# The high halves of k and q made on GpSimd instead of ScalarE, in the attention of a hybrid pooling and attention block

## The reference, cut to what is computed

```python
D_MODEL, SEQ, CHUNK, HEAD_DIM, N_HEADS, LEFT_CHUNKS = 1024, 4096, 64, 64, 8, 8
h = rms_norm(x, norm_gain)                       # x: (1, 4096, 1024) float32
proj = einsum('bsd,de->bse', h, w_in)            # w_in: 1024 x 3072
pool_v, pool_g, q, k, v, attn_g = split(proj)    # 512 columns each
y_pool = multiscale_pool(pool_v, pool_w, pool_scale) * silu(pool_g)
# each chunk of 64 queries reads its own chunk of keys and the 8 before it
s = einsum('bqhd,bkhd->bhqk', qb, kb) / 8 + bias[clip(rel, -64, 64)]
y_attn = einsum('bhqk,bkhd->bqhd', softmax(s), vb) * silu(attn_g)
x = x + einsum('bse,ed->bsd', concat([y_pool, y_attn]), w_out)
out = rms_norm(x, final_norm_gain)
```

## Time and profile before

| | |
|---|---|
| time, median of 3 runs | 1745.24 us (1744.5 to 1748.08) |
| the profiled execution | 1741.65 us, span of its instructions 1739.9 us |
| TensorE matmuls busy | 1629.3 us (94%) |
| VectorE busy | 1057.1 us (61%) |
| ScalarE busy | 837.8 us (48%) |
| GpSimd busy | 693.5 us (40%) |
| mean granted TensorE clock | 0.979 of full |

### The profile page before, as it was taken

The page is one execution under the profiler, slowest core; times in us unless marked ns, Lnnn a source line. Parts: engine busy times, 40 slices in busy tenths (PEclk is TensorE's granted clock), DMA queues, the critical chain, the costliest instruction groups (busy, mean ns, idle before and its releaser), DMA issues. The chain is left out here.

```text
span 1739.9 us, 44264 instructions
## 1 busy us (share of the span) xinstructions
PE 1629.3 (94%) x17920; PEld 1221.2 (70%) x17920; DVE 1057.1 (61%) x2188; ACT 837.8 (48%) x1580; POOL 693.5 (40%) x734
## 2 busy tenths in 40 slices
PE   5999899999999999999967999999999999999986
PEld 2554445558676767777746878898888888888864
DVE  7776587647565556544344665666656666656664
ACT  5554455422121212111124666667666666766674
POOL 3535355311111212000413455555555555555553
PEclk8999999999999999999987999999999999999998
DMA  5665574661634442442834434544434444345331
GB/s 205 217 216 183 209 249 161 221 248 50 219 106 142 175 159 84 161 179 102 230 100 146 135 93 132 151 127 124 126 98 141 145 122 126 104 121 150 96 126 49
DMA packets 131201, 257.87 MB, mean 148 GB/s; under 512 B 15512, under 2 KB 61096, under 8 KB 128952
## 3 DMA queue, kind: packets, MB, share of 16 engines
q1 hardware_dynamic: 127896, 250.07, 43.8%
q10 hardware_dynamic: 2064, 3.67, 0.6%
q0 software_dynamic: 1040, 1.31, 0.4%
HBM read 151.33 MB, written 83.48 MB: 135 GB/s over the span
## 5 line engine op out<-in xcount | busy, mean ns | idle before, releaser
L2089 POOL TENSOR_TENSOR stages<-stages 128x512 f16<-128x512 f32 (+2 forms) x368 | 366.3, 999 | 399.9 <-ACT stages L1925 399.7
L1557 PE MATMUL bank<-middle,weights 128*128 128x128 f16 x1792 | 311.2, 219 | 1.2 <-DVE entry L1213 0.9
L1560 PE MATMUL bank<-middle,weights 128*128 128x128 f16 x1792 | 311.1, 219 | 0.0
L1559 PE MATMUL bank<-middle,weights 128*128 128x128 f16 x1792 | 311.0, 219 | 0.0
L1919 ACT ACTIVATE stages<-bank,log_ps 128x512 f32<-128x512 f32 (+2 forms) x368 | 221.6, 602 | 152.3 <-PE bank L1812 72.9
L1759 DVE CUSTOM_DVE_ANT_0 stages<-bank,stages 128x640 bf16<-128x640 f32 (+4 forms) x256 | 198.2, 774 | 77.2 <-PE bank L1724 77.2
L982 PE MATMUL bank<-middle 128*128 128x256 f16 x784 | 215.3, 275 | 7.4 <-DVE stages L1122 7.4
L984 PE MATMUL bank<-middle 128*128 128x256 f16 x784 | 215.3, 275 | 0.0
L985 PE MATMUL bank<-middle 128*128 128x256 f16 x784 | 215.3, 275 | 0.0
L1925 ACT ACTIVATE stages<-stages 128x512 f16<-128x512 f32 (+2 forms) x368 | 202.8, 551 | 11.7
L1789 PE MATMUL bank<-entry,stages 128*128 128x512 f16 x768 | 188.2, 382 | 2.5 <-DVE stages L1980 2.5
(11 more groups left out here) (147 smaller groups left out, 3611.3 us busy)
## 6 DMA issues: line engine op xcount, KB each, us to landing
entry<-in_x SPq DMA_DIRECT2D x64, 512.0 KB, 3.7
h_ops<-middle SPq DMA_DIRECT2D x16, 1792.0 KB, 6.2
middle<-h_ops SPq DMA_DIRECT2D x112, 256.0 KB, 3.0
middle<-h_ops SPq DMA_DIRECT2D x49, 512.0 KB, 7.0
middle<-middle SPq DMA_DIRECT2D x384, 64.0 KB, 2.0
residual<-entry SPq DMA_DIRECT2D x32, 512.0 KB, 3.1
entry<-residual SPq DMA_DIRECT2D x30, 512.0 KB, 4.2
out<-entry SPq DMA_DIRECT2D x30, 512.0 KB, 4.2
```

The source lines that it names most:

```text
L1557: nc.tensor.matmul(dst, wh, hop3[:, o, 0, kt, :], start=(kt == 0 and s < 2 and pair == 0), stop=False, skip_group_check=True)
L1559: nc.tensor.matmul(dst, wh, hop3[:, o, 1, kt, :], start=False, stop=False, skip_group_check=True)
L1560: mm = nc.tensor.matmul(dst, wl, hop3[:, o, 0, kt, :], start=False, stop=(kt == 3), skip_group_check=True)
L2089: nc.gpsimd.tensor_tensor(p_l[:, h % 2, c + a:c + b], p32[g][:, a:b], p_h[:, h % 2, c + a:c + b], ALU.subtract).then_inc(A["pl_done"], 1)
```

## The change

The call of `kq_hi` is taken out of ScalarE's `head`. GpSimd gets a function `split_hi` that has the same waits and makes the same copy from float32 to float16 as a `tensor_copy`, and calls it in front of `kq_lo`. The places (`split_at`) are the same, behind the third `p_lo` of the head. `kq_lo` waits on `nat_hi` as before, which GpSimd itself now raises. The calls in `q_phase` stay on ScalarE.

```diff
@@ a_phase_act, head @@
                 exponential(t, h, 1)
                 other(t, h, 1)
-                if split_at(t, h):
-                    kq_hi(act, split_at(t, h))
                 if round_at(t, h):
                     branch_hi(*round_at(t, h))
                 other(t, h, 2)
@@ a_phase_pool @@
+            def split_hi(w):
+                pool.wait_ge(A["kq_p"], 2 * w + 2)
+                pool.wait_ge(A["kq_u"], 5 * w + 5)
+                for half in range(2):
+                    at_least(pool, (moved_q if w % 2 else moved_k)[half], 96 * (w // 2))
+                nc.gpsimd.tensor_copy(nat_of(w, 0), cs_flat()).then_inc(A["nat_hi"], 1)
+
             def p_lo(t, h, k):
...
                     if split_at(t, h):
+                        split_hi(split_at(t, h))
                         kq_lo(pool, split_at(t, h))
```

## The result

The changed kernel took 1750.69 us (median of 20 runs, 1745.84 to 1755.6), the kernel before 1745.79 on the same chips (20 runs, 1741.72 to 1751.25). The ratio is 1.0025, with a 95% interval of 1.0016 to 1.0035: 4.4 us slower, 2.8 to 6.1. The forecast was 10.2 slower. The sign is right and 1750.7 lies in the range, but the size is more than twice too large.

What follows compares the result with a forecast made beforehand. TensorE was taken as the bound, matmuls busy 94% of the span. Losses of 2.8, 4.2, 0.8 and 2.4 us at 14 places sum to 10.2, so 1745.2 + 10.2 = 1755.4 us; range 1749 to 1770.

Steps and rivals of the forecast that it cites:

- D: How much later the second split's low half comes on GpSimd: the copy's price plus 0.1, 1.2 us.
- seven plain tiles, D less 0.8 each: At the next tile's first `maxima`, seven places with slack 0.8 us lose 0.4 each, 2.8 together.
- ScalarE's removed copies: 29 copies of about 1.04 us, 30 us busy time off ScalarE, costed at nothing because ScalarE has idle time.
- The chain: Split, low half, six q transfers, next tile's first `maxima`: TensorE loses D less the slack at each of 14 places.
- The price of the copy: One 128x1024 f32-to-f16 copy on GpSimd was taken as 1.1 us, between ends of 0.95 and 2.13.
- the empty cost of the first split: At head 2 the same delay costs nothing: slack 2.3 us, 1.7 in tile 1, before VectorE's third combination of q.
- GpSimd's room behind the second: After the second split GpSimd's third subtraction is late by about 0.15 us, harmless because TensorE reads it a head later.
- four at 1.2 - 0.15 = 1.05: Four tiles where SyncE stalls between q issues have slack about 0.15 us and lose 1.05 each, 4.2 together.
- The low case of the prediction: With a copy of 0.95 us and no SyncE stall recurring, the loss is 12 x 0.25 + 2.1 = 5.1 us.
- B: GpSimd's copy costs as a two-operand instruction or is slowed by VectorE: 16 to 25 us slower, 1761 to 1770; chance 0.17.
- C: The copy on GpSimd stays hidden, total under 3.5 us, time 1745 to 1748 us; chance 0.12.
- E: ScalarE's freed microsecond removes TensorE's 29 waits for VectorE, 17.0 us: 1728 us at most; chance 0.03.

Runs made afterwards that it cites:

- the split wait: Transfers into `qs` first, `maxima` waiting for those four alone: on the changed kernel 1740.39 us, ratio 0.9978; on the kernel before 1739.64 us, 0.9971.
- q_twice: The changed kernel with the high half of q copied twice in a row on GpSimd, a wait between: 1769.94 us, ratio 1.0148 to the kernel before.
- the nops: The changed kernel with 12 instructions that do nothing on SyncE ahead of the attention: ratio 1.0024 to the kernel before.
- both_early: The changed kernel with high and low halves both made on GpSimd in front of the head's third subtraction: 1743.37 us, ratio 0.9982 to the kernel before.
- q_only: The kernel before with only q's high halves, tile 0's included, made on GpSimd; k's stay on ScalarE: 1751.94 us, ratio 1.0045.

## Why the prediction was right in sign and wrong in size

| term | forecast | measured |
|---|---|---|
| D | 1.2 | 1.1 |
| seven plain tiles, D less 0.8 each | 2.8 | 7 x 0.3 = 2.1 |
| tiles 4, 6, 9, 11 and 14 | 5.0 | 3.8 (4.6, 3.6, 3.3), less 0.2 that they lose in before |
| tile 1 | 1.2 | 1.1 |
| tile 2 | 1.2 | 0.1 |
| ScalarE's removed copies | 0 | -1.5 (all in tile 0) |
| last stretch | 0 | 0.2 |
| sum | 10.2 | 5.6 by stages, 4.4 timed |

**What held.** The chain (split, low half, six transfers, `maxima`) is shown by four values of D: 0, 0.5, 1.1 and 2.2 give steady tiles of 53.12, 53.12, 53.42 and 54.52; and by the split wait, which takes the loss away. For D = 2.23 the prediction's sum gives 24.6, and `q_twice` shows 21.1 by stages. The price of the copy, the empty cost of the first split and GpSimd's room behind the second held too. Of the signs it named, ScalarE is 27 us less busy and not 30, the plain tiles are at 53.42 and not at 53.5 or more, and the idle time before `maxima` is 0.13 to 1.41 where 0.4 to 1.2 was forecast.

**What failed first: "I cost this at nothing: the cover is ScalarE's own idle time."** That argument was made in the steady tile, for 29 copies, and one of them is not there. In tile 0 the copy stood ahead of a rounding that VectorE, and behind it TensorE, waited for. Taking it away was worth 1.2 us at the place, in every profile, and 1.5 over the stretch (`tile0_only`, with this copy alone moved, shows 1.0), of which some tenths are scatter. I had asked what the tile's transfers would lose, and not what stood behind the copy on ScalarE.

**What failed second, and cost more: the slack of the irregular tiles.** The sum took "four at 1.2 - 0.15 = 1.05" and 1.2 in tile 2, as if each stall belonged to the transfers it hit and would move with them. It does not: the q8 packet stays at its place in the tile, and the transfers move past it. In tiles 6 and 11 they now start behind it and pay 0.3 like a plain tile, where 1.05 and 0.8 were forecast. In tile 2 the stall was there anyway and swallows the delay, 0.1 for 1.2. In tiles 4 and 9 the packet falls on another issue of the same six, with no slack left to hide it, so that tile 4 cost 1.36 in the first profile. Together these six tiles cost 3.7 for 6.2 forecast, more than half of the error of 4.6; tile 0 is 1.5 of it and the smaller D 0.8, less 0.2 that the last stretch took.

The trace of before could have shown this. It has the packet of tile 6 at 1231.57, 0.4 behind the first q issue, so that a delay of 1.1 puts it 0.7 ahead of that issue; and in tile 3 a packet that began 1.2 ahead of the first issue (1070.60 and 1071.79) slowed none. A smaller slip is in the reading of the slack: it was 0.15 in tiles 4 and 6, but 0.05 in tile 9 and none in tile 14. The low case of the prediction, "if none of the SyncE stalls recurs", gives 5.1, close to the 5.6, but by luck: it goes with a D of 1.05, counts neither tile 0 nor what tile 2 swallows, and in tiles 4 and 9 the stalls do recur.

That the q8 packets cause the slow issues is inferred from their coming together each time; no run took them away. What they load is not known. That their place does not follow the number of SyncE's instructions is shown by the nops, for 12 of them.

**The rivals.** B (two-operand price) is out: 1.04. Its second half, slowed by VectorE, I set aside because "near the splits VectorE's operations read a bank and one SBUF operand"; in tile 0 that is not so, and the low half took 2.98 instead of 2.13, once. C (hidden) is out for the kernel as changed, and true of `both_early`. E in its form (the 29 waits of TensorE) is out: they stayed at 17.0. But its idea, that ScalarE's freed microsecond is worth something, was right in one place.

**Open.** The stages give 5.6 and the timing 4.4, 4.9 and 4.2 for the changed kernel (the last with its nops), with intervals between 1.9 and 7.0; the difference may be chance. The time of `q_only`, and why the split wait shortens tile 0, stay open too.

## What to carry to other kernels

A delay on a chain that feeds the bound costs its length less the slack, tile by tile; measure the slack as the difference between a tile that waits and one that does not, and check which part of the wait the reader needs. A removed instruction costs or gives by what stands behind it on its engine, at each of its places: look at the first and last tile by themselves, not only at the steady one. A stall that comes from outside the kernel's own order need not move with the instruction that it hits. Find where in the tile its source lies, in two or three profiles, and see what the moved instructions will meet there: here the place was the same in the kernel before and in the changed one, and only the length changed.

## What the runs showed of the hardware

- The issue of one 64 KB transfer on SyncE takes about 0.6 us (467 to 607 ns), but 1.0 to 1.9 when a packet of the instruction queue q8 of 0.9 to 1.6 us starts at about the same time (all 15 profiles). Such a packet can also hold back a transfer under way: it landed 4.0 us after its issue instead of 2.0. In the three profiles each of before and of the changed kernel these packets come at the same places, within 0.7 us in tiles 4, 6, 9 and 11, whatever their length.
- The idle time before a matmul can be listed under "issue" though it ends on a transfer's landing. The first `maxima` that came 5.15 to 5.22 after the first of six plain issues start 0.09 after the last landing; those of the plain tiles have 0.13 to 0.20 of idle time.
- A VectorE operation on two SBUF operands and a GpSimd instruction that reads SBUF run one after the other. The same operation (L2037, in before L2039) takes 1.23 us alone, 3.17 when it starts 0.03 behind a low half of 2.12, and 2.30 when it starts 0.91 behind one; in the changed kernel the copy holds it for 1.0, and then it holds the low half, which takes 2.98. That is the exclusive lock that the Trainium skill describes (SBUF — State Buffer, "SBUF: two separate sides"): who starts first keeps the shared ports for the whole instruction. In the three traces it ends 1.07 to 1.09 after the GpSimd instruction that it met, and they agree with this.
- A copy of 128x1024 from float32 to float16 takes 1.04 us on GpSimd and 1.04 on ScalarE.
